# Last output turns, the norms behind them and the final output, by thirds of the tokens

## The reference, cut to what matters

```python
xs = xs + g1 * out                                   # out = (...) @ w_out, 2048 or 1024 rows summed
h  = _modulate(_rms_norm(xs, norm2_g[i]), sh2, sc2)  # x * rsqrt(mean(x*x)+eps) * g * (1+sc) + sh
xs = xs + g2 * _swiglu(h, f_w_in[i], f_w_out[i])     # (silu(h@w_g) * (h@w_u)) @ w_out, 2816 rows summed
...
y_sample = _rms_norm(xs, final_g)
```

## Time and profile before

| | us |
|---|---|
| device time, median of 3 runs | 3627.53 |
| lowest, highest | 3617.62, 3634.0 |
| span of the profiled execution | 3619.9 |
| mixer's last output turn to the next unit's product (839.76 to 922.73) | 82.97 |
| VectorE's last `up` of FFN 1 to its last copy of the output (3532.63 to 3610.03) | 77.40 |

### The profile page before, as it was taken

How to read it: one execution, slowest core, us unless ns; L and a number is a source line. 1 busy time by engine, 2 the same in 40 slices (tenths; PEclk the granted TensorE clock), 3 DMA queues, 4 the chain that set the end, 5 groups by cost and what they waited for, 6 DMA issues and landing times.

```text
span 3619.9 us, 48315 instructions
## 1 busy us (share of the span) xinstructions
PE 3322.2 (92%) x19001; PEld 3230.2 (89%) x19001; DVE 1811.5 (50%) x2947; ACT 924.9 (26%) x1118; POOL 59.3 (2%) x107
## 2 busy tenths in 40 slices
PE   6899999996999999999779888989979999999996
PEld 5898999996999999999779778878769999999995
DVE  6766787877332333323644556555554332333325
ACT  2322111113211111111422445454633111111111
POOL 0000000000000000000000000000000000000001
PEclk6999999998999999999889899999989999999997
DMA  6344433330111111111113100010001111111111
GB/s 199 106 134 127 125 107 106 101 104 26 41 41 41 41 41 41 41 46 38 41 39 108 58 20 26 25 39 13 25 12 33 44 41 41 41 41 44 41 38 53
DMA packets 272777, 210.27 MB, mean 58 GB/s; under 512 B 15214, under 2 KB 243868, under 8 KB 272684
## 3 DMA queue, kind: packets, MB, share of 16 engines
q1 hardware_dynamic: 260908, 163.50, 15.1%
q0 software_dynamic: 11776, 45.39, 3.7%
HBM read 185.10 MB, written 23.76 MB: 58 GB/s over the span
## 4 chain that ended last, share of the span: by engine, by line
PE 80%; DVE 9%; ACT 4%; issue 4%; DMA 2%; SPq 0%; POOL 0%; ACTq 0%; DVEq 0%; POOLq 0%
PE set L492 66%; PE set L791 4%; PE set L779 3%; PE set L526 2%; PE turned L564 2%; ACT tmp L854 1%; DVE soft L1739 1%; DVE pa L1415 1%; DMA tmp<-in_ada_w 1%; DVE acc L1281 1%; ACT pr L854 1%; PE set L578 1%; PE set L587 1%; DVE ptl L1755 1%; PE set L669 1%
## 5 line engine op out<-in xcount | busy, mean ns | idle before, releaser
L492 PE MATMUL set<-hhi,whi 128*128 128x384 f32 x2904 | 675.6, 341 | 22.6 <-DVE hlo L1328 11.3
L492 PE MATMUL set<-hlo,whi 128*128 128x384 f32 x2904 | 671.0, 339 | 0.0
L492 PE MATMUL set<-hhi,wlo 128*128 128x384 f32 x2904 | 670.7, 339 | 0.0
L1433 DVE SCALAR_TENSOR_TENSOR x<-set,mod,x 128x128 f32<-128x128 f32 (+2 forms) x816 | 453.2, 611 | 335.4 <-PE set L492 335.2
L492 PEld LDWEIGHTS set<-hhi,whi 128*128 128x128 f32 x2904 | 523.8, 189 | 27.4 <-issue 14.7
L492 PEld LDWEIGHTS set<-hlo,whi 128*128 128x128 f32 x2904 | 526.2, 189 | 0.0
L492 PEld LDWEIGHTS set<-hhi,wlo 128*128 128x128 f32 x2904 | 525.4, 189 | 0.0
L1273 DVE TENSOR_TENSOR wlo<-wraw,whi 128x1024 fp32r<-128x1024 f32 x211 | 256.9, 1219 | 489.1 <-ACT whi L854 487.1
L854 ACT ACTIVATE whi<-wraw 128x1024 fp32r<-128x1024 f32 x211 | 221.5, 1051 | 745.7 <-PE set L492 718.7
L492 PE MATMUL set<-ghi,whi 128*128 128x384 f32 x1440 | 335.8, 342 | 19.0 <-issue 8.2
L492 PE MATMUL set<-glo,whi 128*128 128x384 f32 x1440 | 333.8, 340 | 0.0
(11 more groups left out here) (185 smaller groups left out, 3688.7 us busy)
## 6 DMA issues: line engine op xcount, KB each, us to landing
wraw<-in_f_w_in SPq DMA_DIRECT2D x176, 256.0 KB, 3.0
adu<-in_ada_w SPq DMA_DIRECT2D x48, 512.0 KB, 6.2
wraw<-in_f_w_out SPq DMA_DIRECT2D x88, 256.0 KB, 2.7
wraw<-in_a_w_in SPq DMA_DIRECT2D x64, 256.0 KB, 4.6
v_scratch<-vst POOLq DMA_DIRECT2D x16, 576.0 KB, 3.1
vld<-v_scratch POOLq DMA_DIRECT2D x16, 576.0 KB, 4.5
q_scratch<-tmp POOLq DMA_DIRECT2D x16, 576.0 KB, 3.1
aldr<-in_ada_w SPq DMA_DIRECT2D x8, 1024.0 KB, 8.9
```

Source lines behind the costliest of these rows:

```text
L492: last = nc.tensor.matmul(ps[:, b, 0:cols], w, m[:, b * cols:(b + 1) * cols], start=(i == 0 and p == 0), stop=(i == n - 1 and p == 2))
L1433: last = v.scalar_tensor_tensor(dst, src, k.mod[:, gate + n, c:c + 1], dst, ALU.mult, ALU.add)
```

## The change

The 1152 tokens are three thirds of 384 (one PSUM bank each; the first third holds the 128 context tokens and 256 latent ones). Three places change: mixer to FFN 0, FFN 0 to attention, FFN 1 to the output.

- The last output turn is done third by third. A job is now three (or two) feature tiles of one third, nine jobs in place of eight. Its first two jobs start with the first hidden tile alone. In the FFNs the last `up` product and its two parts are also made by thirds (`last_up`).
- Squares are made for each third on ScalarE and summed by GpSimd (`third_sums`). One fp32 product of ones with the sum (`mean_square`) gives the mean square of a third on all partitions; ScalarE takes the root into `rstd`, VectorE the reciprocal. Column sums, diagonal matrix and spreading product go.
- The norm of a third: VectorE `(x * gain) * rstd`, ScalarE adds the shift and rounds, VectorE makes the rest in one instruction. The next two products (`third_in_jobs`) run third by third, first unit and then second unit in each.
- Both next weight units are split inside the norm of the second third.
- The output: 8 scaled tiles a third, transposes of four tiles at a time into one bank, copies shared by ScalarE (four of six) and VectorE (two of six), and one DMA per 128 tokens with whole rows of 4 KB.

```diff
+TRIOS = ((0, 1, 2), (3, 4, 5), (6, 7))
+def third(t):
+    return slice(t * CH, (t + 1) * CH)
+def third_parts(t):
+    return [(0, CTX, 0), (CTX, CH, 1)] if t == 0 else [(t * CH, t * CH + CH, 1)]
...
@@ class Products (TensorE) @@
+    def mean_square(self, t):
+        k, b = self.k, self.T.odd()
+        self.eng.wait_ge(k.t_free[b], self.T.half())
+        self.eng.wait_ge(k.sq3_used, 21 * self.N + 7 * t + 7)
+        self.nc.tensor.matmul(k.tps[b][:, 0:CH], k.ones[:], k.acc[:, third(t)], start=True, stop=True
+                              ).then_inc(k.t_done, 1)
+        self.T.step()
+    def third_tile(self, out, n, t, mh, ml, which):
+        nc, slot = self.nc, self.U.odd(n // 4)
+        for a in which:
+            wh, wl = self.weight(slot, a * 512 + n % 4 * P)
+            for p, (w, m) in enumerate(((wh, mh), (wh, ml), (wl, mh))):
+                last = nc.tensor.matmul(out, w, m[:, a, third(t)], start=(a == 0 and p == 0),
+                                        stop=(a == 1 and p == 2))
+        return last
+    def last_out_jobs(self, mh, ml, first_ready, second_ready):
+        k, J = self.k, self.J
+        self.unit_ready()
+        self.eng.wait_ge(*first_ready)
+        ps = [self.open()]
+        self.eng.wait_ge(k.freed[J.odd(1)], J.half(1))
+        ps.append(k.sets[J.odd(1)])
+        for g in range(2):
+            for j, n in enumerate(TRIOS[g]):
+                if n == 4:
+                    self.unit_ready(1)
+                self.third_tile(ps[g][:, j, 0:CH], n, 0, mh, ml, (0,))
+        self.eng.wait_ge(second_ready[0], second_ready[1])
+        for g in range(2):
+            for j, n in enumerate(TRIOS[g]):
+                last = self.third_tile(ps[g][:, j, 0:CH], n, 0, mh, ml, (1,))
+            self.close(last)
+        for t in range(3):
+            if t:
+                self.eng.wait_ge(second_ready[0], second_ready[1] + second_ready[2] * t)
+            for g, trio in enumerate(TRIOS):
+                if t == 0 and g < 2:
+                    continue
+                out = self.open()
+                for j, n in enumerate(trio):
+                    last = self.third_tile(out[:, j, 0:CH], n, t, mh, ml, (0, 1))
+                self.close(last)
+                if t and g == 1:
+                    self.mean_square(t - 1)
+        self.U.step(2)
+    def third_in_jobs(self):
+        k, nc, J = self.k, self.nc, self.J
+        ps = [self.open()]
+        self.eng.wait_ge(k.freed[J.odd(1)], J.half(1))
+        ps.append(k.sets[J.odd(1)])
+        for t in range(3):
+            for u in range(2):
+                if t == 0:
+                    self.unit_ready(u)
+                for n in range(DT):
+                    if u == 0:
+                        self.eng.wait_ge(k.lo3_ready, 24 * self.N + 8 * t + n + 1)
+                    wh, wl = self.weight(self.U.odd(u), n * P)
+                    for p, (w, m) in enumerate(((wh, k.hhi), (wh, k.hlo), (wl, k.hhi))):
+                        last = nc.tensor.matmul(ps[u][:, t, 0:CH], w, m[:, n, third(t)],
+                                                start=(n == 0 and p == 0), stop=(n == DT - 1 and p == 2))
+                if t == 2:
+                    self.close(last)
+            if t == 0:
+                self.mean_square(2)
+        self.U.step(2)
+        self.N += 1
@@ mixer_turn, ffn_turn, ffn(0), attention @@
+            self.last_out_jobs(k.ghi, k.glo, (k.a_ready, self.A.at(-1)), (k.a_ready, self.A.at(), 0))
...
+            self.last_out_jobs(k.ghi, k.glo, (k.a_ready, self.A.at()), (k.ul3_ready, 3 * self.M + 1, 1))
...
-        self.statistics()
-        self.first_in_jobs()
+        self.third_in_jobs()
@@ program, the end @@
-        self.statistics()
-        for n in range(DT):
-            pe.wait_ge(k.y_ready, n + 1)
-            for g in range(3):
-                self.turn([k.tmp[:, n % 4, (3 * g + b) * P:(3 * g + b + 1) * P] for b in range(3)])
+        for t in range(3):
+            if t == 1:
+                self.mean_square(2)
+            for n in range(2):
+                pe.wait_ge(k.y_ready, 8 * t + 4 * n + 4)
+                for b in range(3):
+                    self.turn([k.yt[:, t % 2, 4 * n + f, b * P:(b + 1) * P] for f in range(4)])
@@ class Activations (ScalarE) @@
+    def third_squares(self, t, trio):
+        k = self.k
+        self.J.step()
+        self.eng.wait_ge(k.freed[self.J.odd(-1)], self.J.half(-1) + 1)
+        for n in trio:
+            if n == 0:
+                dst = k.acc[:, third(t)]
+            else:
+                a = 7 * t + n - 1
+                dst = k.tmp[:, 2, third(a % 3)]
+                if 21 * self.N + a >= 3:
+                    self.eng.wait_ge(k.sq3_used, 21 * self.N + a - 2)
+            self.act(dst, k.x[:, n, third(t)], ACT.Square).then_inc(k.sq3_ready, 1)
+    def third_root(self, t):
+        k, b = self.k, self.T.odd()
+        self.eng.wait_ge(k.t_done, self.T.at(1))
+        self.act(k.rstd[:, third(t)], k.tps[b][:, 0:CH], ACT.Sqrt, scale=1.0 / D, bias=k.eps[:, 0:1]
+                 ).then_inc(k.t_free[b], 1)
+        self.T.step()
+    def third_norm(self, t, shift, lo, hi):
+        k = self.k
+        for n in range(lo, hi):
+            i = 8 * t + n
+            hi_part, xg = k.hhi[:, n, third(t)], k.tmp[:, 1, third(i % 3)]
+            self.eng.wait_ge(k.xg_ready, 24 * self.N + i + 1)
+            for p, q, c in third_parts(t):
+                r = self.act(hi_part[:, p - t * CH:q - t * CH], xg[:, p - t * CH:q - t * CH], ACT.Identity,
+                             bias=k.mod[:, shift + n, c:c + 1])
+            r.then_inc(k.hi3_ready, 1)
+    def boundary(self, shift, doubled):
+        for trio in TRIOS:
+            self.third_squares(0, trio)
+        for t in (1, 2):
+            self.third_squares(t, TRIOS[0])
+            self.third_squares(t, TRIOS[1])
+            self.third_root(t - 1)
+            self.third_norm(t - 1, shift, 0, 2)
+            if t == 2:
+                self.split(double=doubled)
+            self.third_squares(t, TRIOS[2])
+            if t == 2:
+                self.split()
+            self.third_norm(t - 1, shift, 2, DT)
+        self.third_root(2)
+        self.third_norm(2, shift, 0, DT)
+        self.N += 1
+    def y_rows(self, t):
+        k, T = self.k, self.T
+        for n in range(2):
+            for b in range(3):
+                if b % 2 == 0:
+                    self.eng.wait_ge(k.t_done, T.at(1))
+                    self.act(k.yst[:, 3 * t + b, n * 512:(n + 1) * 512], k.tps[T.odd()][:]
+                             ).then_inc(k.t_free[T.odd()], 1)
+                T.step()
@@ last turn of an FFN, ScalarE @@
+    def last_up(self):
+        k = self.k
+        self.J.step()
+        for t in range(3):
+            if t < 2:
+                self.eng.wait_ge(k.up3_ready, 2 * self.M + t + 1)
+            else:
+                self.eng.wait_ge(k.freed[self.J.odd(-1)], self.J.half(-1) + 1)
+            self.act(k.ghi[:, 1, third(t)], k.tmp[:, 1, third(t)]).then_inc(k.uh3_ready, 1)
+        self.M += 1
@@ after the last turn of ffn(1), ScalarE @@
+        for trio in TRIOS:
+            self.third_squares(0, trio)
+        for t in (1, 2):
+            self.third_squares(t, TRIOS[0])
+            self.third_squares(t, TRIOS[1])
+            self.third_root(t - 1)
+            self.third_squares(t, TRIOS[2])
+        self.y_rows(0)
+        self.third_root(2)
+        self.y_rows(1)
+        self.y_rows(2)
@@ class Elementwise (VectorE) @@
+    def third_out(self, gate, t, trio):
+        k, v = self.k, self.nc.vector
+        self.eng.wait_ge(k.mm_done, self.J.at(1))
+        ps = k.sets[self.J.odd()]
+        for j, n in enumerate(trio):
+            for lo, hi, c in third_parts(t):
+                dst = k.x[:, n, lo:hi]
+                last = v.scalar_tensor_tensor(dst, ps[:, j, lo - t * CH:hi - t * CH],
+                                              k.mod[:, gate + n, c:c + 1], dst, ALU.mult, ALU.add)
+        self.free(last)
+    def third_rstd(self, t):
+        k, b = self.k, self.T.odd()
+        self.eng.wait_ge(k.t_free[b], self.T.half() + 1)
+        self.T.step()
+        self.nc.vector.reciprocal(k.rstd[:, third(t)], k.rstd[:, third(t)]).then_inc(k.rc3_ready, 1)
+    def third_lo(self, t, shift, lo, hi):
+        k, dve, v = self.k, self.eng, self.nc.vector
+        if lo == 0:
+            dve.wait_ge(k.rc3_ready, 3 * self.N + t + 1)
+        for n in range(lo, hi):
+            if n < DT:
+                i = 8 * t + n
+                if i >= 3:
+                    dve.wait_ge(k.lo3_ready, 24 * self.N + i - 2)
+                xg = k.tmp[:, 1, third(i % 3)]
+                for p, q, c in third_parts(t):
+                    r = v.scalar_tensor_tensor(xg[:, p - t * CH:q - t * CH], k.x[:, n, p:q],
+                                               k.gain[:, n, c:c + 1], k.rstd[:, p:q], ALU.mult, ALU.mult)
+                r.then_inc(k.xg_ready, 1)
+            if n >= 2:
```

(115 more changed lines are left out.)

178 lines of the change are left out of this document (105 added, 73 removed).

## The result

| | before | after |
|---|---|---|
| device time, median, same chip | 3630.77 us (4 runs) | 3594.88 us (4 runs) |
| lowest, highest | 3617.62, 3635.76 | 3585.39, 3600.31 |
| span of the profiled execution | 3619.9 | 3594.5 |

What follows compares the result with a forecast made beforehand. TensorE, busy 92% of the span, was taken as the bound, so only its waits and half clock counted. Terms -0.9 - 2.1 - 7.3 = -10.3 us, put on the median 3627.5, gave 3617 us, range 3598 to 3640.

Steps and rivals of the forecast that it cites:

- The change can move no more than those, the start of three last turns, and a small wait behind each: Upper limit on the gain: "those" are all of TensorE's gaps, together 105 us, 2.9% of the span.
- Sum -10.3: Forecast total over the three changed places: -0.9 - 2.1 - 7.3 = -10.3 us against a span of 3619.9.
- A: Mixer to FFN 0, first output matmul to the third unit's product: 82.97 us before, forecast 82.1, -0.9.
- B: FFN 0 to attention, from VectorE's last `up` to the third unit's product: 86.54 us before, forecast 84.4, -2.1.
- C: FFN 1 to output, from the last `up` to the last copy's end: 77.40 us before, forecast 70.1, -7.3.
- the tail: Stretch of the span behind the output's last copy, 9.9 us, forecast to stay as it is.
- Reciprocal 2.7: VectorE's reciprocal of 384 columns, three times a boundary, priced at 2.7 us from rows of one and nine columns.
- Rival 1: Root and reciprocal are cheap: a reciprocal of 0.55 us, -28 us in all, 3600 us; chance 0.2.
- Rival 2: GpSimd's adds of squares are the bound, at 2.2 us each: +26 us, 3654 us; chance 0.13.
- The sign named for it: Forecast is wrong if TensorE waits more than 1 us for GpSimd at the product with ones.
- Rival 3: GpSimd and VectorE disturb each other: later thirds' adds take 1.6 us instead of 1.0; -6, 3621 us; chance 0.1.
- Rival 4: ScalarE reloads the root's table after each group of squares, 1.28 us a load: -2.5, 3625 us; chance 0.05.

## Why the prediction missed

- **"The change can move no more than those, the start of three last turns, and a small wait behind each"**: this step failed. It took a matmul's 0.176 us as fixed and every ordinary turn as untouched. The count in equal windows shows the pace itself moving, by a tile of one word that the diff adds among the tiles and that I did not price at all. It made 0.41% by its own experiment, 15 us beside the schedule's 11. The 25.4 us of span confirm it: 13.5 in FFN 0's ordinary turns.
- **Sum -10.3.** Right for the schedule, 10.9 us by the experiment without the move (6.5 to 15 by its interval), but with luck. That run's own trace has A 81.35 (-1.6), B 83.58 (-3.0), C 68.53 (-8.9) and the tail +3.4, in all -10.1: the three distances gave 3.2 us more than forecast, and the tail took 3.4.
- **A -0.9, measured -3.8.** TensorE's wait for the split was forecast at 17.6 us and was 17.35. The half clock at the start was charged with 2.6 us, from 18 matmuls; here the clock rose after 9, at 842.9, and 9 x (0.32 - 0.17) is 1.3. So the first reciprocal starts 22.1 us in, where 20.8 + 2.6 = 23.4 had been the sum. In the run without the move the half clock lasted longer, the reciprocal starts at 23.7, and A is 81.35 against the 82.1 of the forecast. Why it lasts longer in some runs is open.
- **B -2.1, measured -2.8.** The start 1.64 us behind `up` (forecast 1.7), `csk` as releaser of the third split, and the end at 83.71 (84.4) all came as worked out.
- **C -7.3, measured -8.9**, longest wait 6.1, under the 7 forecast; last copy 68.5 behind `up` instead of 70.1.
- **The tail, left at 9.9, was 13.25**, and took a third of C's gain back. I named three DMAs of 512 KB at the very end, but their transfer is not it: the last byte moves 4.4 us after the last copy, where it was 4.6 before. The growth lies behind the last byte, where no engine and no DMA shows anything: 8.9 us to the end of the span, in all ten runs of the changed kernel, against 5.2 to 5.3 in all four of the kernel before. What fills it stays open.
- **Reciprocal 2.7, measured 2.553; add 1.0, measured 1.048.** The slope between 1 and 9 columns carried to 384 within 6%. Rival 1 is out by that: it wanted 0.55. With a stand-in of 0.61 in their place A, B and C lose 12.6 us, where the rival counted 17.5. Rival 2 is out by the add's 1.048. The sign named for it did show, though: TensorE waits 0.55 us for the adds at the first product with ones, but 1.5 at the second in A of the run without the move and in B of the kernel run again. It stood 17.3 us for the split all the same.
- **Rival 3** is half right. GpSimd and VectorE do disturb each other: beside VectorE's scaled tiles an add takes 1.28 us, where the mean of all is 1.05 (the rival said 1.6), and VectorE loses 0.76 us an add. It is worth at most the 6.2 us of the short adds over the kernel, and it did not lift the time to 3621. The Trainium skill, "GPSIMD Engine Reference", section "Key points", has GpSimd share its SBUF interfaces with VectorE and contend with its instructions that have two SBUF inputs; the rows agree, 5.84 against 4.32 us for eight such instructions.
- **Rival 4** is out. There are 22 table loads, as before. The one load in this stretch stands ahead of the first root; the squares and the second root that follow show none:

```profile
3533.86 1.28 ACT L963 ACT_TABLE_LOAD   x1
...
3549.84 0.53 ACT L963 ACTIVATE tmp<-x 128x384 f32<-128x384 f32 x1 [0.61 <-POOL acc L2093]
3550.27 0.56 ACT L963 ACTIVATE rstd<-turned,eps 128x384 f32<-128x384 f32 x1
```

- **The range.** Its lower end came from the cheapest reciprocal. It held no term for the 92% of the span that I called untouched, and there 1% of pace is 30 us.

## What to carry to other kernels

Where one engine is full for most of the span, count its instructions in equal windows as well as its busy share. Two stretches of the same work at full clock with other counts (3695 and 3705 here, visible before the change) say that something sets the pace that no wait shows, and here a new tile of one word moved it. Before pricing a diff, list what it does to the places of tiles, and try a layout move on its own. And when a wait has only changed its owner, look at what is queued ahead of the instruction that ends it: the split's place gave another 7.5 and 9 us by the distances of its two runs.

## What the runs showed of the hardware

TensorE's pace with clock 1.00 and no wait, in matmuls per 650 us (FFN 0, FFN 1), by the bytes per partition by which the activations were moved:

| moved by | kernel | counts | ratio |
|---|---|---|---|
| 0 | before | 3695, 3705 | |
| 0 | before, run again | 3695, 3695 | 0.9998 |
| 0 | after, not moved | 3695, 3695 | 0.997 |
| 64 | before | 3752, 3681 | 0.9959 |
| 64 | after | 3752, 3681 | 0.9906 |
| 64 | after, run again | 3681, 3723 | 0.9921 |
| 64 | after, other order of the splits | 3752, 3752 | 0.9906 |
| 64 | after, no reciprocals | 3723, 3752 | 0.9879 |
| 128 | after | 3752, 3752 | 0.9875 |
| 192 | after | 3752, 3752 | 0.9858 |
| 192 | after, short adds | 3752, 3752 | 0.9839 |
| 192 | after, other order of the splits | 3752, 3752 | 0.9824 |
| 192 | before | 3751, 3752 | 0.9889 |
| 256 | after | 3695, 3695 | 0.9958 |

At 128 and 192 the pace is 173.3 ns in every window, at 0 and 256 175.9 (once 175.4), and at 64 it is 173.3, 174.6 or 176.6, constant within a stretch (in steps of 50 us it holds from the first ordinary turn of an FFN to the last) and often another in the next. The counts are of the profiled execution, the ratios of all executions of a kernel. The pace changed only across stretches in which TensorE had stood and the clock had been at half; that it is drawn anew there is what the windows suggest, not what an experiment has shown. Which of the tiles must lie where (the activations against the split weights, or against what VectorE, ScalarE and the DMAs write meanwhile) stays open too: every run moved the whole region at once.
